# Two transformer blocks on one core: modulation rows by VectorE, a new order of projections, a tenth place for expert weights and a last sum in PSUM

## What is computed

```python
def first_block(x, c, ...):
    shift, scale, gate = split(silu(c) @ w_ada + b_ada, 3)
    h = rmsnorm(x, norm_g) * (1 + scale) + shift
    (qm, km, vm, om, zm, im, fm, qa, ka, va, za, gm, ga) = split(h @ w_in)   # 14 344 columns
    qm, km = silu(causal_dwconv([qm, km]))
    hm = head_rmsnorm(sigmoid(om) * mlstm(qm, km, vm, im, fm)) * silu(zm)
    ha = head_rmsnorm(diff_attention(qa, ka, va, lam, rel_bias)) * silu(za)
    y = sigmoid(gm) * (hm @ w_proj_m) + sigmoid(ga) * (ha @ w_proj_a)
    return rmsnorm(x + gate * (y @ w_out), final_g)

def second_block(x, c, ctx, c_ctx, ...):
    sh1, sc1, g1, sh2, sc2, g2 = split(silu(c) @ w_ada + b_ada, 6)   # the same for c_ctx
    s_f, s_b = context_states(rms(ctx) @ w_in ...)                   # keys and values alone
    hx = rms(x) * (1 + sc1) + sh1
    x_b, x_c, x_x, q, k, v, g = split(hx @ w_in)
    mix = [x_b * conv3(x_c * x_x), silu(g) * groupnorm(retention(q, k, v, s_f, s_b))] @ w_out
    x = x + g1 * rms(mix)
    h = rms(x) * (1 + sc2) + sh2
    # each of 16 experts: its 32 best tokens, silu(xs @ w_gate) * (xs @ w_up) @ w_down, summed back
    return x + g2 * rms(expert_choice_ffn(h))
```

## Time and profile before

| | |
|---|---|
| median of 3 runs | 1648.84 us (1648.56 to 1649.22) |
| the profiled execution's own time | 1648.3 us |
| its span, first to last instruction | 1646.3 us |
| mean granted clock of TensorE in it | 0.884 |
| busy: TensorE, VectorE, ScalarE, GpSimd | 1264.4, 571.3, 426.0, 35.8 us |
| bytes moved by DMA | 551.66 MB |

### The profile page before, as it was taken

How to read it: one execution, slowest core, us unless ns; L and a number is a source line. 1 busy time by engine, 2 the same in 40 slices (tenths; PEclk the granted TensorE clock), 3 DMA queues, 4 the chain that set the end, 5 groups by cost and what they waited for, 6 DMA issues and landing times.

```text
span 1646.3 us, 18014 instructions
## 1 busy us (share of the span) xinstructions
PE 1264.4 (77%) x7278; PEld 684.2 (42%) x7278; DVE 571.3 (35%) x955; ACT 426.0 (26%) x644; POOL 35.8 (2%) x60
## 2 busy tenths in 40 slices
PE   3999999999999989877656665756665666665764
PEld 1877877777787779731111111111111111111111
DVE  2676446667657784731101101110110110111012
ACT  1657336677545664420000000000000000000000
POOL 1000000001000000000000000000000000000000
PEclk8999999999999999978888778787888878788687
DMA  9565547676666553789999999999999999999995
GB/s 352 193 242 210 191 162 267 229 269 242 248 240 216 184 174 125 292 348 429 429 427 428 428 427 429 428 428 427 429 426 429 427 428 429 427 429 427 428 427 236
DMA packets 87425, 551.66 MB, mean 335 GB/s; under 512 B 6104, under 2 KB 6424, under 8 KB 58672
## 3 DMA queue, kind: packets, MB, share of 16 engines
q1 hardware_dynamic: 84256, 541.09, 80.7%
q0 software_dynamic: 2800, 9.14, 1.7%
q10 hardware_dynamic: 288, 0.30, 0.1%
HBM read 549.41 MB, written 1.09 MB: 334 GB/s over the span
## 4 chain that ended last, share of the span: by engine, by line
PE 51%; DMA 34%; DVE 9%; ACT 3%; issue 2%; SPq 0%; POOL 0%; DVEq 0%; POOLq 0%; ACTq 0%
PE ps L531 48%; DMA b<-in_w_down 32%; DVE b L1286 4%; PE ps L535 3%; ACT b L952 2%; DMA b<-in_w_ada 2%; DVE b L1926 1%; DVE b L1894 1%; DVE b L1896 1%; DVE b L1303 1%; POOL b L1961 0%; DVE b L1296 0%; SPq L457 0%; DVE b L1317 0%; DVE b L1902 0%
## 5 line engine op out<-in xcount | busy, mean ns | idle before, releaser
L531 PE MATMUL ps<-b,b 128*32 128x512 f32 (+3 forms) x6922 | 1204.7, 554 | 303.8 <-DMA b<-in_w_up 105.7
L531 PEld LDWEIGHTS ps<-b,b 128*32 128x32 f32 (+2 forms) x6922 | 637.2, 157 | 824.3 <-issue 294.6
L1286 DVE TENSOR_TENSOR b<-b,b 128x1024 fp32r<-128x1024 f32 (+6 forms) x261 | 283.8, 1088 | 213.0 <-ACT b L952 198.3
L952 ACT ACTIVATE b<-ps 128x512 f32<-128x512 f32 (+3 forms) x180 | 98.2, 545 | 891.9 <-PE ps L531 581.0
L952 ACT ACTIVATE b<-b 128x1024 fp32r<-128x1024 f32 (+4 forms) x223 | 221.7, 994 | 268.7 <-PE ps L531 153.0
L1916 DVE TENSOR_TENSOR b<-b,ps 128x512 f32<-128x512 f32 x16 | 11.0, 688 | 402.4 <-issue 385.8
L1926 DVE TENSOR_TENSOR b<-b,ps 128x1024 f32<-128x1024 f32 x28 | 34.2, 1221 | 332.1 <-PE ps L531 332.1
L535 PE MATMUL ps<-b,b 128*128 128x128 f32 x356 | 71.3, 333 | 66.8 <-DVE b L1317 26.9
L535 PEld LDWEIGHTS ps<-b,b 128*128 128x128 f32 x356 | 47.9, 173 | 125.7 <-DVE b L1317 37.7
L1286 DVE TENSOR_TENSOR b<-ps,b 128x512 f32<-128x512 f32 (+7 forms) x63 | 34.5, 548 | 11.7 <-ACT b L954 4.7
L1961 POOL TENSOR_TENSOR b<-b,b 128x1 f32<-128x1 f32 (+3 forms) x15 | 13.1, 873 | 1117.6 <-DVE b L1296 1117.6
(11 more groups left out here) (51 smaller groups left out, 158.5 us busy)
## 6 DMA issues: line engine op xcount, KB each, us to landing
b<-in_w_gate SPq DMA_DIRECT2D x64, 2048.0 KB, 40.7
...
b<-in_w_in SPq DMA_DIRECT2D x74, 1024.0 KB, 6.3
b<-in_w_ada SPq DMA_DIRECT2D x36, 1024.0 KB, 8.3
b<-in_w_proj_m SPq DMA_DIRECT2D x8, 1024.0 KB, 7.4
b<-in_w_out SPq DMA_DIRECT2D x8, 1024.0 KB, 4.9
b<-in_w_proj_a SPq DMA_DIRECT2D x4, 1024.0 KB, 5.0
```

The costliest lines, as they stand in the source:

```text
L531: return e.matmul(o, lhsT, rhs, start=start, stop=stop, skip_group_check=True)
L952: e.activation(o, i, f, bias=bias, scale=scale).then_inc(mark[0], 1)
L1286: e.tensor_tensor(o, a, b, op).then_inc(mark[0], 1)
```

## The change

- **Modulation on VectorE.** Of the 28 chunks the first eight (row R1) stay on TensorE. The other 20 are now products with a scalar per partition, summed by VectorE into `ADA_ACC`: one `scalar_tensor_tensor` of 128x2048 for a chunk (two of 128x1024 for four of them, one `tensor_scalar` for a row's first piece). A matmul with a matrix of ones (`ada_sum`) then sums over the partitions, three times in all. Two chunks each stand in slots 9 to 12, one each in 13 to 23 and one in 25. R3 comes before R2.
- **The ring.** A chunk's load stands behind one more pair of halves.
- **Start.** `ADA0` comes as two halves of 4 MB, the first for the input's rows 0 to 511; modulation and projections begin with that half. V0 comes before Q0 and the two slots are interleaved, so the first four halves need only these rows; V and Q or K trade places up to slot 7, and the work beside them moves by one slot.
- **Bias.** GpSimd writes 2 MB (every head's row 128 times, in four DMAs) and reads 1 MB back with a stride that gives the bias in its final order; `bias_turn` and ScalarE's copies are gone.
- **Second block.** CB comes before G2; the convolution on VectorE moves from slots 42 and 43 to 41 and 42 and the group norm the other way; the transposes of the retention (`RF`) go from (42, 2) to (43, 2), those of its queries (`QF`) from (38, 0) to (38, 2). WP0 and WP1 take the convolution's rows first.
- **Experts.** Chunk 8 goes to a tenth place, used once (`E_ONCE`, `EX`), and its load waits for `v_x2` instead of `v_h2`; chunk 9 takes the place that chunk 8 had. The row `GG2` (0.5 MB) is loaded after chunk 8 has been used, where before it was loaded beside slot 35. `late` is loaded later too.
- **End.** TensorE carries `ACC` into PSUM by a matmul with the identity during the last expert and adds the last expert on top; ScalarE squares and VectorE scales from PSUM.

```diff
-NADA = 28
-ADA_LAST = {7: "R1", 11: "R2", 19: "R3", 27: "R4"}
-ADA_STEP = {(a + 1, 3): a for a in range(NADA)}
+NADA_PE = 8
+ADA_STEP = {(a + 1, 3): a for a in range(NADA_PE)}
+for _a, _step in enumerate(((9, 0), (9, 2), (10, 0), (10, 2), (11, 0), (11, 2), (12, 0), (12, 3),
+                            (13, 3), (14, 3), (15, 3), (16, 3),
+                            (17, 3), (18, 3), (19, 3), (20, 3), (21, 1), (22, 1), (23, 1), (25, 3))):
+    ADA_STEP[_step] = [ADA_STEP[_step], NADA_PE + _a] if _step in ADA_STEP else NADA_PE + _a
+ADA_SUM = {(13, 0): "R3", (17, 0): "R2", (26, 0): "R4"}
...
-    for step, a in ADA_STEP.items():
-        after.setdefault(place[step], []).append(a)
+    for step, chunks in ADA_AT.items():
+        for a in chunks:
+            after.setdefault(place[step] + 1, []).append(a)
...
-    ("Q0", "T", "w_in", QM, "H"), ("V0", "N", "w_in", VM, "H"), ("K0", "T", "w_in", KM, "H"), ("V1", "N", "w_in", VM + W, "H"),
+    ("V0", "N", "w_in", VM, "H"), ("Q0", "T", "w_in", QM, "H"), ("V1", "N", "w_in", VM + W, "H"), ("K0", "T", "w_in", KM, "H"),
...
-    ("CX", "T", "w_in_2", CX2, "H2"), ("G2", "N", "w_in_2", G2, "H2"), ("CB", "T", "w_in_2", CB2, "H2"),
+    ("CX", "T", "w_in_2", CX2, "H2"), ("CB", "T", "w_in_2", CB2, "H2"), ("G2", "N", "w_in_2", G2, "H2"),
...
+            def ada(a):
...
+                e.wait_ge(*landed(("ada", a)))
...
+                    if k % KD == 0:
+                        ts(acc, slot[:, kk, :], cst[:, k:k + 1], None, ALU.mult, to=S("v_ada") if kk == kt - 1 else None)
+                    else:
+                        stt(acc, slot[:, kk, :], cst[:, k:k + 1], acc, ALU.mult, ALU.add, to=S("v_ada") if kk == kt - 1 else None)
...
+            def ada_sum(name):
+
+                begin(name)
+                e.wait_ge(S("v_ada"), {"R3": 8, "R2": 12, "R4": 20}[name])
+                for n in range(2 if name == "R2" else 4):
+                    ins = mm(ps[32 * n:32 * n + 32, 7, :], ones, ADA_ACC[name][:, n * W:(n + 1) * W], True, True)
...
-            for k in range(7):
-                ada0(k)
+            for k in range(0, KD, 2):
+                ada0(0, k)
             ring_load(0)
-            ada0(7)
-            for i in range(1, len(LOADS)):
+            for k in range(0, KD, 2):
+                ada0(1, k)
+                if k == 2:
+                    ring_load(1)
+            for i in range(2, len(LOADS)):
                 ring_load(i)
...
-            load(toep.rearrange("(h j) -> h j", h=AH), brow, "toep_in")
-            e.wait_ge(S("toep_in"), 16)
-            load(BREV, bass.AP(toep.tensor, 0, [[1, P], [2 * T, AH], [1, T]]), "brev_in")
+            for i in range(4):
+                load(toep.rearrange("(h i r j) -> h i r j", h=AH, i=4, r=P // 4)[:, i], brow.unsqueeze(1).broadcast_to([AH, P // 4, 2 * T]), "toep_in")
+            e.wait_ge(S("toep_in"), 64)
+            load(BIAS, bass.AP(toep.tensor, P - 1, [[2 * T - 1, P], [P * 2 * T, AH], [1, T]]), "bias_turned")
...
+            e.wait_ge(S("v_x2"), NT)
+            expert_load(E_ONCE)
             e.wait_ge(S("v_h2"), NT)
-            expert_load(8)
-            for c in range(E_SLOTS, NE * NCH):
-                e.wait_ge(S("p_use"), c - E_SLOTS + 1)
+            expert_load(9)
+            for c in range(E_SLOTS + 1, NE * NCH):
+                e.wait_ge(S("p_use"), expert_before(c) + 1)
                 expert_load(c)
...
+            def carry(t, nd):
+                mm(ps[:, LAST_AT[t] + nd, :], ident, ACC[:, t, nd * W:(nd + 1) * W], True, False)
...
-                    a_ = ACC[:, t, n * W:(n + 1) * W]
-                    tt(a_, a_, ps[:, (6, 2)[t] + n, :], ALU.add, to=S("v_last"))
+                    e.wait_ge(S("a_osq"), 2 * t + n + 1)
+                    ns = slice(n * W, (n + 1) * W)
+                    tt(FG2[:, t, ns], ps[:, LAST_AT[t] + n, :], GG2[:, ns], ALU.mult)
```

More of the change, by code:

```diff
@@ L135, in _halves @@
         n = 8 if name in ("PM0", "PM1") else 4
[L136 removed]
+        if name in ("V0", "WO0", "WP0"):
             other = SLOTS[s + 1][0]
[L138 removed]
             for i, (which, a) in enumerate(((name, 0), (other, 0), (name, 2), (other, 2))):
                 for j in range(2):
[L141 to L142 removed]
+                    add(which, a + j, a + j == 0, a + j == 3, (s + i // 2, 2 * (i % 2) + j))
+        elif name not in ("Q0", "WO1", "WP1"):
             for kp in range(n):
@@ L425, in ring_free @@
                 return S("v_lo"), 2 * n + 2
-            if n in ADA_LAST:
-                return full(ADA_LAST[n])
-            return S("p_ada"), n + 1 - sum(1 for a in ADA_LAST if a < n)
+            if n >= NADA_PE:
+                return S("v_ada"), n - NADA_PE + 1
+            return full("R1") if n == NADA_PE - 1 else (S("p_ada"), n + 1)
         def landed(what):
@@ L492, in _ @@
             expert_load(0)
-            e.wait_ge(*full("CBb"))
+            e.wait_ge(*full("G2b"))
             expert_load(1)
@@ L744, in _ @@
                     continue
-                if (s, c) == (0, 0):
+                if s == 0 and c < 3:
+                    for k in ((0, 1, 2, 3), (4, 5, 6), (7,))[c]:
+                        ada0(1, k)
+                if (s, c) == (1, 2):
                     begin("BROW")
@@ L844, in _ @@
                     flip_pair("RF1", RY, 2)
-                if (s, c) in ADA_STEP:
-                    ada(ADA_STEP[s, c])
+                for a in ADA_AT.get((s, c), ()):
+                    if a < NADA_PE:
+                        ada(a)
+                if (s, c) in ADA_SUM:
+                    ada_sum(ADA_SUM[s, c])
             for t in range(NT):
@@ L930, in _ @@
                 for t in range(NT):
-                    b0 = 2 if t == 1 and x == NE - 1 else 6
-                    if t == 1 and x < NE - 1:
+                    last = x == NE - 1
+                    if t == 1 and not last:
                         e.wait_ge(S("v_acc0"), x + 1)
@@ L1046, in _ @@
                 hi(g)
-            e.wait_ge(*free("R0F"))
-            for q in range(4):
-                if q == 2:
-                    e.wait_ge(S("v_mod"), 1)
+            e.wait_ge(*free("R0F0"))
+            for q in range(2):
                 modulate_hi(f"XT{q}", HTH, GS, SH)
@@ L1099, in _ @@
                     act(AJ[:, P:T], ps[:, 6, P:T], ACT.Square, accum=assq[:, AH + h:AH + h + 1], to=free(f"AV{h}"))
+                if 13 <= s < 21 and c == 3:
+                    h = s - 13
+                    e.wait_ge(*full(f"FL{h}"))
+                    copy(AT[h % 2], ps[:, 6, 0:3 * P], to=free(f"FL{h}"))
                 if 12 <= s < 20 and c == 3:
@@ L1107, in _ @@
                             to=S("a_exp") if m else None)
-                if 13 <= s < 21 and c == 3:
-                    h = s - 13
-                    e.wait_ge(*full(f"FL{h}"))
-                    copy(AT[h % 2], ps[:, 6, 0:3 * P], to=free(f"FL{h}"))
                 if 19 <= s < 23 and c == 0:
@@ L1818, in _ @@
                         tt(v, v, ps[:, USE[n][0], :], ALU.mult, to=free(n))
-                if (s, c) == (43, 1):
+                if (s, c) == (42, 1):
+                    for t in range(NT):
+                        e.wait_ge(*free(f"RV{t}"))
+                    reduce(gmean, RY4, ALU.add)
+                    ts(gmean, gmean, 1.0 / RD, None, ALU.mult)
+                    tt(RY4, RY4, gmean.unsqueeze(2).broadcast_to([P, NT * RH, RD]), ALU.subtract)
+                if (s, c) == (42, 2):
                     for i in range(2):
@@ L2007, in _ @@
             rows_out(MODT[0], 4, 3 * D)
+            load(late, dram["late"], "late_in")
             e.wait_ge(*full("PA1b"))
@@ L2032, in _ @@
                 power(12 + t, hsq[:, t:t + 1])
+            e.wait_ge(S("p_use"), E_ONCE + 1)
+            load(GG2, dram["mods"][4 * D:5 * D].partition_broadcast(P), "gg_in")
             for t in range(NT):
```

338 lines of the change are left out of this document (176 added, 162 removed).

## The result

The changed kernel takes 1635.74 us (median of 4 runs, 1634.05 to 1638.96) against 1649.03 us before, a ratio of 0.9921 (95% interval 0.9908 to 0.9933). It is 13.3 us faster where 42.8 were forecast, and the time lies outside the range. The profiled execution has a span of 1632.8 us.

What follows compares the result with a forecast made beforehand. The prediction took TensorE as the bound first (VectorE tight from 500 to 700 us), then the expert stream's DMA and a tail. Terms summed to 42.8 us off the profiled 1648.3, plus 0.5 to the median: 1606 us, range 1597 to 1622.

Steps and rivals of the forecast that it cites:

- second rival: Bias's traffic, 3 MB on GpSimd's queue beside the ring: a stall of 10.9 us, 1617 us; chance 0.12.
- start: Kernel's beginning: modulation and projections start on the first half of `ADA0`; gain 4.5 us, bounds nothing to 8 us.
- stall at 98 us: ScalarE's wait for a weight and TensorE's idle time and slow matmuls, taken as gone: 5 us, bounds +5.5 and -5.4.
- turning: Slots 5 and 7: the four `bias_turn` matmuls leave TensorE, which is full there; gain 3.5 us.
- chunks: Twenty modulation chunks leave TensorE and three sums come back: net 17.2 us, bounds 5 to 19 us.
- queries' transposes: Second block: TensorE's 4.21 us stop at 600.34 us goes, other work coming first; gain 5.5 us, bounds 3 and 6.
- slots 41 to 44: Second block: the 3.67 us stall at 672.37 us is moved and not removed; zero, bounds 3 us either way.
- tenth place: Experts: the stream runs one chunk ahead, 4.9 us, less `GG2`'s 1.2 us; net 3.7 us, bounds -1.2 and 3.7.
- tail: Kernel's end: 13.4 us after the last chunk's landing instead of 16.8; gain 3.4 us, bounds 2 and 4.
- First rival: VectorE becomes the bound in slots 13 to 25; 12 chunks give nothing, 12.8 us: 1619 us; chance 0.14.
- Third rival: Experts: late chunk 2 pushes the whole stream and the gap only moves; 4.9 us lost, 1611 us; chance 0.08.
- Fourth rival: Slower than before: all 20 chunks lie on the path, 47 us: 1653 us; chance 0.03.

Runs made afterwards that it cites:

- sixteen copies: Changed kernel, but 16 copies of each head's row written (256 KB instead of 2 MB), bias read back in eight loads of 16 partitions: 1608.82 us.
- late read: Changed kernel with rows made on 32 partitions, 32 copies (512 KB) written, and the bias's read held back until the gates' transposes in slot 7: 1605.68 us.

## Why the prediction was wrong

By its own sum, with the run that undid each term:

| term | forecast | measured |
|---|---|---|
| bias's writes | nothing (the stall's bound of -5.4 and the second rival had 10.9) | -26.9 (changed kernel less sixteen copies) |
| start, stall at 98 us, turning | 4.5 + 5 + 3.5 = 13.0 | 7.4 with sixteen copies, 9.1 with the late read (first `lo` of slot 9 at 157.67 and 155.95 us, before at 165.07) |
| chunks | 17.2 | 22.9 |
| queries' transposes | 5.5 | 7.9 when undone, 5.8 by the rows of before |
| slots 41 to 44, tenth place | 0 + 3.7 | 2.8 (tenth place when undone: 4.8) |
| tail | 3.4 | 3.6 |

With 7.4 and 5.8 these add up to 15.6 us, where 13.3 were measured.

**The step that failed** is the price of the bias's traffic: the sum has nothing for it. The second rival had the mechanism, the place and the wait (ScalarE for weights at 90 to 110 us), and was off in size: it took three times what 1 MB had cost, less the added lead, 10.9 us; 26.9 were lost. The row it scaled was a read onto 128 partitions, 7.3 us for 1 MB; the new transfer is a write from 8 partitions, and 2 MB of it take 42.9 us. The only transfer of that kind in the trace of before is the write of 16 KB, which landed in 3.1 us, too small to show a rate; the bound was taken from one of another kind. The rule of taking turns, cited there from the Trainium skill (DMA: Bandwidth & Descriptors, Queues, rings and completion order), did not mislead: the engines did move about as many packets with data, and bytes, of each queue. But the half was reckoned from the full rate, when the engines spent 87% of their time on the slow packets.

**The rest of the forecast stood.** With the traffic out of the way the same change takes 1605.7 to 1608.8 us; 1606 was forecast. But that is partly luck, since terms were wrong inside it on both sides. The stall at 98 us went, as forecast: TensorE runs through it in the run with the old bias, and the ring's order alone gives 6.7 us in the kernel before. Yet start, stall and turning together gave 7.4 us and not 13.0 with sixteen copies, as TensorE waits in slot 7 instead, 2.98 us and a clock of 0.86 in that slot; and 9.1 us with the late read, where the wait is 0.63 us and slot 8 runs at a clock of 0.90 (17.18 us of it, so 1.7 us). The chunks and the transposes gave 8 us more than forecast: four of the chunks take 1.9 us of TensorE and not 1.07, and the low clock behind the transposes' stall lasts longer than the rows of before showed.

**First rival** (VectorE the bound in slots 13 to 25): only a trace of it. TensorE idles 1.14 us in slot 24, 3.1 us over slots 8 to 28, and the chunks still give 22.9 us. **Third rival** (the tenth place gives nothing): not so, the tenth place gives 4.8 us. But something takes part of it back: from the first `lo` of slot 41, behind which the reordering of the second block lies, to the last landing it is 997.6 us before and 994.8 in the changed kernel, 2.8 us where 3.7 were forecast. The late chunk 2 is 0.8 us of that, by the run that swaps the places; the share of `GG2` in the stream (1.2 us by its bytes) was tested by no run. **Fourth rival** (all chunks on the path, 1653 us): the forecast gave it 0.03, and its size comes without the ring's lead, 1646.5 us, though by another path: not VectorE's work in a slot, but the loads behind the chunk. The forecast wrote that VectorE's wait for a chunk costs nothing, but looked only at the load in front of the chunk, not at the loads behind it, which wait until VectorE has let go of its place. The cover for that was one line of the diff, and it was not priced.

What stays open: the start was tested by no run. By the timeline it is about 4.4 us (the fifth half at 52.64 against 57 us), but in the later runs, whose start is the same, that half begins 0.3 to 2.0 us later. With all chunks back on TensorE and sixteen copies, the kernel is 4.6 us ahead of the one before at slot 29 (460.4 against 465.0 us), and how these divide among start, turning and the waits of slot 7 was only argued from the timelines.
